# 160 of 544 tokens through gathered expert rows instead of 128, 32 of them packed four heads side by side, with longer runs for what is kept in DRAM

## The reference, cut to what matters

```python
q = einsum('td,de->te', xt, w_q).reshape(t, 8, 2, 128)     # 8 heads, 2 sides
s = einsum('thpc,hpkc->thpk', q, sub_keys)                 # 128 scores a side
s1, i1 = top_k(s[:, :, 0], 16); s2, i2 = top_k(s[:, :, 1], 16)
top_s, j = top_k(s1[..., :, None] + s2[..., None, :], 16)  # of 256 pairs
e = i1[j // 16] * 128 + i2[j % 16]                         # 16 experts a head
gate = softmax(top_s)
act = gelu(einsum('td,thkd->thk', xt, u_experts[e]))
out = einsum('thk,thkd->td', gate * act, v_experts[e])
```

## Time and profile before

| | |
|---|---|
| median of 3 runs | 1608.98 us (1602.33 to 1609.36) |
| the profiled execution | 1603.43 us, its span 1601.3 us |
| TensorE busy | 96% of the span |
| VectorE, ScalarE, GpSimd busy | 76%, 41%, 51% |
| moved by DMA | 407.60 MB, 255 GB/s over the span |
| granted TensorE clock, mean | 0.983 |

### The profile page before, as it was taken

One profiled execution on the slowest core, in us unless ns is written; L12 is line 12 of the kernel. 1 busy time (PEld: TensorE's weight loads), 2 busy tenths in 40 slices (PEclk: granted clock), 3 DMA queues, 4 the chain that ended last, 5 costly groups with the idle time before them and its releaser, 6 DMA issues.

```text
span 1601.3 us, 26951 instructions
## 1 busy us (share of the span) xinstructions
PE 1538.5 (96%) x9360; PEld 1505.2 (94%) x9360; DVE 1223.4 (76%) x2594; ACT 649.9 (41%) x838; POOL 813.6 (51%) x497
## 2 busy tenths in 40 slices
PE   6998889999999989999999998999999999999996
PEld 6997879998999989899999998999999999999996
DVE  6998983788999996777777630677777777787775
ACT  5244443343333344566666523333333333333332
POOL 5686533336667756666676675244344444343301
PEclk9999989999999999999999999999999999999999
DMA  4321212227767767999999997789998998999841
GB/s 165 96 89 53 83 45 102 66 90 250 227 225 245 276 221 245 351 370 363 352 372 372 353 399 265 245 324 355 341 350 326 335 326 318 353 344 345 323 167 56
DMA packets 149503, 407.60 MB, mean 255 GB/s; under 512 B 12224, under 2 KB 75968, under 8 KB 147648
## 3 DMA queue, kind: packets, MB, share of 16 engines
q1 hardware_dynamic: 89776, 215.27, 39.5%
q0 software_dynamic: 36864, 134.23, 22.3%
q10 hardware_dynamic: 22800, 57.42, 9.2%
HBM read 349.99 MB, written 56.89 MB: 254 GB/s over the span
## 4 chain that ended last, share of the span: by engine, by line
PE 86%; DVE 6%; DMA 5%; ACT 2%; issue 1%; POOL 0%; DVEq 0%; SPq 0%; ACTq 0%
PE ps_unit L750 32%; PE ps_unit L810 18%; PE ps_misc L810 18%; PE ps_unit L567 13%; DMA acts_dram<-act_ring 3%; PE ps_misc L784 2%; DMA raw<-stream 1%; DVE mov_lo L1150 1%; PE ps_misc L710 1%; PE ps_unit L642 1%; ACT gates L1061 1%; DVE hid L1270 1%; PE ps_unit L697 0%; DMA hid<-x_t 0%; DMA rows<-u_rows,expert 0%
## 5 line engine op out<-in xcount | busy, mean ns | idle before, releaser
L446 POOL TENSOR_TENSOR w_lo<-raw,w_hi 128x1024 fp32r<-128x1024 f32 x172 | 417.1, 2429 | 300.5 <-ACT w_hi L865 188.8
L750 PE MATMUL ps_unit<-mov_hi,w_hi 128*128 128x416 f32 x1024 | 366.7, 358 | 8.5 <-POOL w_lo L446 8.5
L531 POOL DMA_INDIRECT rows<-v_rows,expert x128 | 207.9, 1624 | 318.0 <-DVE sums L1358 309.2
L750 PE MATMUL ps_unit<-mov_hi,w_lo 128*128 128x416 f32 x1024 | 362.6, 354 | 0.0
L750 PE MATMUL ps_unit<-mov_lo,w_hi 128*128 128x416 f32 x1024 | 360.3, 352 | 0.0
L865 ACT ACTIVATE w_hi<-raw 128x1024 fp32r<-128x1024 f32 x300 | 315.7, 1053 | 89.8 <-ACT act_ring L1033 59.9
L1085 ACT ACTIVATE prod_hi<-prod 128x416 fp32r<-128x416 f32 x128 | 70.7, 552 | 367.1 <-PE ps_misc L810 365.8
L1544 DVE TENSOR_TENSOR prod_lo<-prod,prod_hi 128x416 fp32r<-128x416 f32 x128 | 75.8, 592 | 173.9 <-ACT prod_hi L1085 173.9
L750 PEld LDWEIGHTS ps_unit<-mov_hi,w_hi 128*128 128x128 f32 x1024 | 194.0, 189 | 11.3 <-ACT w_hi L865 5.2
L750 PEld LDWEIGHTS ps_unit<-mov_lo,w_hi 128*128 128x128 f32 x1024 | 194.4, 190 | 2.6
L750 PEld LDWEIGHTS ps_unit<-mov_hi,w_lo 128*128 128x128 f32 x1024 | 193.8, 189 | 1.8
(11 more groups left out here) (213 smaller groups left out, 2739.8 us busy)
## 6 DMA issues: line engine op xcount, KB each, us to landing
raw<-stream SPq DMA_DIRECT2D x300, 512.0 KB, 4.5
acts_dram<-act_ring ACTq DMA_DIRECT2D x128, 208.0 KB, 5.2
gates_dram<-gates ACTq DMA_DIRECT2D x13, 2048.0 KB, 10.7
gates_in<-gates_dram SPq DMA_DIRECT2D x16, 1664.0 KB, 14.8
acts_in<-acts_dram SPq DMA_DIRECT2D x32, 832.0 KB, 7.5
hid<-x_t SPq DMA_DIRECT2D x4, 544.0 KB, 8.0
rows<-u_rows,expert POOLq DMA_INDIRECT x128, 6.9
rows<-v_rows,expert POOLq DMA_INDIRECT x128, 7.6
```

Of the source, the lines that this page charges most:

```text
L446: nc.gpsimd.tensor_tensor(w_lo[:, j, :], raw[:, j, :], w_hi[:, j, :].bitcast(F32), ALU.subtract).then_inc(lo_made, 1)
L531: nc.gpsimd.indirect_dma_start(out=rows[:, n % ROWS_RING, :], out_offset=None, in_=table, in_offset=bass.IndirectOffsetOnAxis(ap=expert[:, ...
L750: last = nc.tensor.matmul(dense_psum(j), w[:, j, k * P:(k + 1) * P], m[:, k, 0:DENSE], start=(k == 0 and n == 0), stop=(k == KC - 1 and n ...
```

## The change

- `GATHERED` is 160: `DENSE` is 384, so 3 dense tiles in place of 4, 12 gate groups in place of 13, and matmuls of 384 columns.
- The 32 new gathered tokens (512 to 543; the other 128 are now 384 to 511) are packed: each stands on 4 groups of 32 partitions, and each group holds 2 of the 8 heads. So they need 32 slots more (`SLOTS` = 160). Their scores come in a fourth PSUM bank, `best_pairs` runs for them once with 2 tiles, after the dense heads. For their dots `x_rows` is overwritten by `x_rows_x` after slot 127. Their weighted rows are added into `sums_x`, first of all v slots (`value_slot`), and at the end the 4 groups are brought together by 4 DMAs and three additions.
- `EARLY_HEADS` is 2, `U_BEFORE` 15, 5 dots in each of 12 gate groups in place of 6 in each of 13; `U_AFTER` stays 5. One `soften` for all tokens in place of two. `fetched_by` follows: 35 dots before the gates, 60 in them, 65 after.
- Activations are spilled in pairs of units from a ring of 4 (runs of 3 KB), gates are loaded for 16 units, in 3 pieces of 4 groups (runs of 2 KB), one group ahead; `product` runs 4 units ahead in place of 3.
- The starting values of `sums` and `sums_x` are transposed after the gates instead of before the u units.

```diff
-GROUP = 8
+GROUP = 16
+QUARTERS = GROUP // QUARTER
+GATE_PIECES = 3
-GATHERED = 128
+GATHERED = 160
+PACKED = GATHERED - P
+PARTS = P // PACKED
+PACKED_HEADS = HEADS // PARTS
-U_BEFORE = 14
+U_BEFORE = 15
-SLOTS = HEADS * TOPK
+WHOLE = HEADS * TOPK
+SLOTS = WHOLE + PACKED_HEADS * TOPK
-EARLY_HEADS = 1
-DOTS_A_GROUP = 6
-DOTS_EARLY = (HEADS - EARLY_HEADS) * DOTS_A_HEAD
+EARLY_HEADS = 2
+DOTS_A_GROUP = 5
+DOTS_EARLY = (HEADS - EARLY_HEADS + 1) * DOTS_A_HEAD
+MADE_AHEAD = AHEAD + 1
+def value_slot(m):
+    return (m + WHOLE) % SLOTS
 def fetched_by(u):
-    n = u - FIRST_U - 8
-    if n < -2:
+    n = u - FIRST_U - 3
+    if n < 3:
         return 0
-    heads = DOTS_A_HEAD * max(7 * n // (RING * U_BEFORE - 6), 0)
-    groups = DOTS_A_GROUP * max(u - FIRST_U - RING * U_BEFORE - 2, 0) // RING
-    return min(min(heads, DOTS_EARLY) + groups, SLOTS) + ROWS_RING
+    early = DOTS_EARLY * min(max(n - 10, 0), RING * U_BEFORE - 10) // (RING * U_BEFORE - 10)
+    groups = DOTS_A_GROUP * min(max(n - RING * U_BEFORE, 0), RING * GTS) // RING
+    late = (SLOTS - DOTS_BEFORE) * max(n - RING * (U_BEFORE + GTS), 0) // (RING * U_AFTER - 3)
+    return min(early + groups + late, SLOTS) + ROWS_RING
...
-            def load_gates(group, s):
-                g = gates_dram[:, :, bass.ds(GROUP * group, GROUP), :].rearrange("g p e t -> p g (e t)")
+            def load_gates(group, s, piece):
+                part = slice(piece * GTS // GATE_PIECES, (piece + 1) * GTS // GATE_PIECES)
+                g = gates_dram[part, :, bass.ds(GROUP * group, GROUP), :].rearrange("g p e t -> p g (e t)")
...
+                for q in range(quarters):
                     sp.wait_ge(prod_made, GROUP * group + QUARTER * (q + 1))
-                    load_acts(2 * group + q + 2, q)
-                    if q and gates_too:
-                        load_gates(group + 2, s)
+                    load_acts(QUARTERS * group + q + 2, q % 2)
+                    if q < GATE_PIECES and gates_too:
+                        load_gates(group + 1, 1 - s, q)
...
+            for j in range(RING):
+                u_unit(N_U // RING - U_AFTER, j)
+                if j == 1:
+                    pe.wait_ge(g_took, BATCHES * GTS)
+                    for bank, at in ((0, DENSE), (2, T - P)):
+                        for k in range(KC):
+                            last = nc.tensor.transpose(ps_misc[:, bank + k // 4, (k % 4) * P:(k % 4 + 1) * P],
+                                                       hid[:, k, at:at + P], ident[:])
+                        last.then_inc(rows_turned, 1)
...
             def u_unit(lap, j, first=False, between=None):
                 split_high(FIRST_U // RING + lap, j + 2)
-                if not first:
-                    act.wait_ge(act_saved[(j + 2) % RING], 16 * (lap + j // 2))
+                if not first and j % 2 == 0:
+                    act.wait_ge(act_saved[j // 2], 16 * lap)
...
-                nc.scalar.activation(act_ring[:, j % 2], dense_psum(j), ACT.Gelu).then_inc(act_took, 1)
-                spill(lap, j)
+                nc.scalar.activation(act_ring[:, j], dense_psum(j), ACT.Gelu).then_inc(act_took, 1)
+                if j % 2:
+                    spill(lap, j // 2)
...
             def dot(n):
                 dve.wait_ge(row_in[n % ROWS_RING], 16 * (n // ROWS_RING + 1))
+                if n == WHOLE:
+                    dve.wait_ge(row_used, WHOLE)
+                    step(nc.vector.tensor_copy(x_rows, x_rows_x[:]))
+                    settle()
...
+            best_pairs(scores_x, PACKED_HEADS, lambda t: TILES * HEADS + t, lambda s: ij_x[:, s],
+                       lambda at: dots_of(HEADS - EARLY_HEADS, at))
+            experts(WHOLE, SLOTS, ij_x[:, 0], ij_x[:, 1])
+            soften()
```

More of the change, by code:

```diff
@@ L398, in _ @@
             for s in range(2):
-                load_gates(s, s)
+                for piece in range(s, GATE_PIECES, 2):
+                    load_gates(0, 0, piece)
                 for j in range(RING):
@@ L707, in head_scores @@
                     pe.wait_ge(scores_took, head)
[L708 to L712, removed]
+                for side in range(2):
+                    for t, at in enumerate(TILE_AT):
+                        nc.tensor.matmul(ps_misc[:, t // 2, (t % 2) * 256 + side * P:(t % 2) * 256 + side * P + P],
+                                         q_ring[:, 2 * s + side, at:at + P], keys[:, 2 * head + side, :],
+                                         start=True, stop=True)
+                    part, at = (head % PARTS) * PACKED, (head // PARTS) * 2 * NKEYS + side * NKEYS
+                    last = nc.tensor.matmul(ps_misc[part:part + PACKED, 2, at:at + NKEYS],
+                                            q_ring[:, 2 * s + side, PACKED_AT:T], keys[:, 2 * head + side, :],
+                                            start=True, stop=True)
                 last.then_inc(scores_done, 1)
-            def key_view(head, s, side):
-                return keys[:, bass.ds(2 * head + side, 1), :].rearrange("p a n -> p (a n)")
             first_queries()
@@ L734, in _ @@
                     head_scores(0, 0)
-            with pe.Fori(1, N_Q // RING) as lap:
+            for lap in range(1, N_Q // RING):
                 for j in range(RING):
@@ L1005, in _ @@
                 if j == 1:
-                    for n, dst in enumerate((x_rows_in, sums)):
+                    for n, dst in enumerate((x_rows_in, x_rows_x)):
                         act.wait_ge(rows_turned, n + 1)
@@ L1052, in _ @@
                     u_unit(lap, j)
-                    if lap == 1 and j == 0:
-                        exponents(0, DTILES, TILES)
-            exponents(1, 0, DTILES)
+            act.wait_ge(shifted, 1)
+            nc.scalar.activation(gate[:], gate[:], ACT.Exp).then_inc(exp_made, 1)
             for j in range(RING):
@@ L1369, in best_pairs @@
                 at_of = [best_at[:, t, s] for t, s in rows_of]
-                top_of = [tops[:, (t0 + t) * HEADS + head] for t in tiles]
+                top_of = [tops[:, top_at(t)] for t in tiles]
                 settle_for_max()
@@ L1547, in _ @@
             dots_to(SLOTS)
-            for v in range(AHEAD):
+            for v in range(MADE_AHEAD):
                 product(v)
@@ L1561, in _ @@
             for v in range(N_V):
-                if v < N_V - AHEAD:
-                    product(v + AHEAD)
+                if v < N_V - MADE_AHEAD:
+                    product(v + MADE_AHEAD)
                 if v == FIRST_SUM - 1:
                     dve.wait_ge(gelu_made, 1)
-                    dve.wait_ge(gate_made, 2)
-                    nc.vector.tensor_tensor(weight[:], gelu[:],
-                                            gate[:, DTILES * HEADS:].rearrange("p h k -> p (h k)"),
-                                            ALU.mult).then_inc(weight_made, 1)
+                    dve.wait_ge(gate_made, 1)
+                    whole = slice(DTILES * HEADS, TILES * HEADS)
+                    packed = slice(TILES * HEADS, GATE_ROWS)
+                    for a, b, of in ((0, WHOLE, whole), (WHOLE, SLOTS, packed)):
+                        last = nc.vector.tensor_tensor(weight[:, a:b], gelu[:, a:b],
+                                                       gate[:, of].rearrange("p h k -> p (h k)"), ALU.mult)
+                    last.then_inc(weight_made, 1)
+                    dve.wait_ge(rows_in_made, 4)
                     dve.wait_ge(weight_made, 1)
```

239 lines of the change are left out of this document (148 added, 91 removed).

## The result

| | |
|---|---|
| changed kernel, median of 7 runs | 1618.2 us (1611.48 to 1625.1) |
| kernel before, 7 runs beside them | 1602.33 us (1597.83 to 1609.36) |
| ratio | 1.0088, 95% interval 1.0063 to 1.0113 |
| span of the profiled execution | 1614.4 us (before 1601.3) |

A forecast was written before the change was run, and what follows sets the result against it. TensorE, 96% busy, was taken as the bound, with transfers near full as a second. v beginning at 1014 plus 558 gave 1572, profiled execution 1574, named median 1577, 32 us less; range 1547 to 1609.

The forecast's parts named there:

- The matmuls: All u and v matmuls: 384 columns take 14.6 ns less each, over 6144 matmuls 89.7 us saved.
- u units alone: Stage of 60 u units before the gates: 273 us, so the gates begin at 616.5 (before 612.3).
- the hole: TensorE's wait while GpSimd stands for the experts, then does eight fetches and a split: 17 us, before 3.6.
- The gates: Stage of 12 gate groups: 21.0 us each, matmuls and bytes both near that bound, 252 us in all; ScalarE's spill waits go.
- The last 20 u units: Stage before v: 65 dots left instead of 15, GpSimd as good as fully busy, last dot at 1002; matmul saving buys nothing.
- The rival of a slow clock there: Last u laps: TensorE idles 3 us a unit and falls to half clock, 17 us more, 1594; chance 0.13.
- The chain behind the last dot: Between last u dot and first v matmul: products, splits, unit 127 and a GELU take 12 us; v starts at 1014.
- The v stage: v and the end: 594.3 less 44.9 for matmuls plus 9 for transfers and bursts, 4.25 us a unit, 558 us.
- The sign that I had named: v stage: the forecast is wrong if TensorE has holes there that end at `prod`, `prod_lo` or `w_lo`.
- The packed rows' last additions: End of v stage: 3 + 1 operations of some 1.2 us fall into units without row sums and cost nothing.
- The cap near 365 GB/s: Rival: transfers cap the v stage, 4.48 us a unit, 36 us in place of 9, 1617; chance 0.2.
- The rival of the third piece: v stage: third gate piece late, or VectorE fails to hide; 25 to 30 us more, 1605; chance 0.12.

The follow-up runs named there:

- u_later: v_order, with GpSimd waiting for the experts and sending the first eight fetches after splitting u unit FIRST_U + 9 instead of + 6: 1564.63 us.
- before_pairs: Kernel before, with only activations spilled in pairs of units from a ring of 4 and read back in longer runs: 1594.65 us, ratio 0.9939.
- u_spread: v_order, with 8 dots in place of 5 in each head's routing, so 44 dots instead of 65 in the last u laps: 1554.46 us.
- v_order: Changed kernel, with the last two weight loads of a v lap issued after the next quarter's activation and gate loads instead of before: 1574.77 us, ratio 0.9818.
- v_ahead3: Changed kernel, with product running 3 units ahead, as before the change, instead of 4: 1573.6 us, one run.
- v_short_stream: Changed kernel, with v weight units from the third lap on loaded only in 576 of 1024 columns: 1591.12 us, one run.
- v_gates_first: Changed kernel, with all three pieces of the next group's gates sent at the first quarter of a group: 1630.75 us, one run.

## Why the prediction was wrong

*The matmuls* were right: 173.2 ns for 173.6 where nothing holds TensorE up.

*u units alone*: 276.8 for 273. The mechanism of the hole is as told. Timeline of GpSimd in the changed kernel, beside the earlier trace rows:

```profile
369.72 2.40 POOL L480 TENSOR_TENSOR w_lo<-raw,w_hi 128x1024 fp32r<-128x1024 f32 x1 [2.40 <-issue]
381.81 1.13 POOL L567 DMA_INDIRECT rows<-u_rows,expert  x1 [9.69 <-ACT w_hi L913]
...
390.72 0.94 POOL L567 DMA_INDIRECT rows<-u_rows,expert  x1 [0.30 <-issue]
391.68 7.02 POOL L480 TENSOR_TENSOR w_lo<-raw,w_hi 128x1024 fp32r<-128x1024 f32 x3
```

GpSimd has split at 372.1 and stands 9.7 us; then come the eight fetches and the split. The experts were made at 381.2, for my 379.5. TensorE's hole was 14.0 us, for my 17. `u_later` moved this wait and got 10 us: the hole is 4.0 us there. That the stage still took 4 us more than forecast lies partly in matmuls 175.3 ns apart for 173.6 (2.5 us); the rest is open.

*The gates*: 250 for 252. I had said that the waits for spills go; `before_pairs` puts 9 us on that part of the change.

*The last 20 u units*: 141 for 145.5, at 386 GB/s. That rows left over set the pace is shown by `u_spread`, 28 us for 21 rows. Whether GpSimd's time (7.3 us a unit) or the bytes are the nearer limit stays open: both fall with the rows, and no run moved one alone. GpSimd was not "as good as fully busy", with 105 of the 140 us, and from 874 to 1004 us VectorE waited 48.6 us for rows to land while the queues carried 399 GB/s; that leans to the bytes. The rival of a slow clock there was half right, at a mean of 0.87, but the stage was no longer than forecast. The chain behind the last dot came as told, 12 us: dots end at 1003.7, v begins at 1015.6.

*The v stage* is the step that failed: "I take 4.25, nearer to 400 [...] and the rest is for bursts". The bytes and the rate hold (393 GB/s at 4.16 us a unit in `v_order`), and VectorE's share nearly does (3.9 us busy a unit for 3.8). What I priced at 9 us was the lead of the loads, and its loss cost 40 (598.8 for the 558.4 of `v_order`): by the gaps in the two traces about 26 us in holes, the rest in the slow clock behind them, for which I had set nothing in this stage. I had worked out that the third piece of gates has 4 units, 17 us, against a landing time of 14.8. The trace of the changed kernel has 7 us at that place. I counted from the condition that SyncE waits for (`prod_made`) and left out what stands ahead of it in SyncE's order, four weight loads of 14 us. The timeline of SyncE in the kernel before shows them too:

```profile
1196.91 15.32 SPq L370 DMA_DIRECT2D raw<-stream  x4
1212.70 0.38 SPq L377 DMA_DIRECT2D acts_in<-acts_dram  x1
1213.30 0.38 SPq L382 DMA_DIRECT2D gates_in<-gates_dram  x1
```

And I read "`product` runs 4 units ahead in place of 3" in the diff without a price: it asks for activations and gates one unit sooner while their issue hangs on the weight splits. `v_ahead3` and `v_order` each lengthen that lead on their own, by one unit and by two, and each takes the whole loss away. The sign that I had named came true: TensorE's holes end at `w_lo`.

That `v_order` comes to 558.4, just the forecast's 558, is partly luck. Its units take 4.16 us, so the 9 us were not spent on them. They went elsewhere: "The packed rows' last additions [...] fall into units without row sums, so nothing" was wrong too. In `v_order` they hold VectorE ahead of the last weight split, and TensorE stands 5.6 us for it (in the changed kernel as well, at 1578.6). VectorE, then TensorE:

```profile
1531.27 3.59 DVE L1675 TENSOR_TENSOR rows<-rows 32x1024 f32<-32x1024 f32 x3
1534.89 1.21 DVE L1677 CUSTOM_DVE_ANT_0 rows<-rows 32x1024 f32<-32x1024 f32 x1
...
1536.04 1.21 DVE L1568 TENSOR_TENSOR w_lo<-raw,w_hi 128x1024 fp32r<-128x1024 f32 x1
```

```profile
1537.30 0.69 PE L860 MATMUL ps_unit<-prod_hi,w_hi 128*128 128x384 f32 x1 [5.60 <-DVE w_lo L1568]
```

And from the last start of a v matmul to the end pass 17.6 us, for 13.1 before; no run says why. A smaller slip: 1574 and 5.6 give 1580 for the median, and I named 1577.

*The rivals.* The cap near 365 GB/s would have given 1617, almost the time measured, and it is refuted: `v_order` carries 393 at a share of 1.00, and `v_short_stream` keeps the late gates at 325. In the changed kernel 364 GB/s was the result of VectorE's standing still, not its cause. By the Trainium skill (DMA: Bandwidth & Descriptors, "Specifications"), about 358 GB/s is a core's limit to HBM; with one core at work, 393 over 400 us disagrees. The rival of the third piece (7 boundaries of 4 us, chance 0.12) was the nearest: about 26 us of holes did come, at the starts of groups. It left out the activations, which came late as well, and the slow clock behind each hole.

## What to carry to other kernels

A prefetch has as much lead as lies between its issue and its use, and in an in-order queue the issue comes when everything ahead of it has stopped waiting: read both times in the trace before saying that a transfer is hidden. Running a consumer further ahead takes lead from its inputs; here one unit of 4.2 us made the difference between 1574 and 1618 us, a kernel about 30 us faster than before or one 16 us slower, with 6 to 10% to spare on VectorE instead of 22% and the queues near full. In this stage the slow clock behind the holes cost about half of what the holes themselves did; a price for a wait of TensorE has to include it. A DMA rate that looks like a ceiling can be the echo of a stall: ask whether it stays when bytes are taken away.

## What the runs showed that I had not expected

The 16 DMA engines carried 393 GB/s for 400 us beside a TensorE without a hole. A load queue near its limit is sensitive to order alone: `v_gates_first` takes 53 us more than `v_order` for the same bytes (v 611.7 for 558.4). After the hole of 14 us TensorE ran 4.7 us at a granted clock of about 0.5 (1.2 GHz). Timeline of TensorE, changed kernel:

```profile
394.20 0.66 PE L789 MATMUL ps_unit<-mov_hi,w_hi 128*128 128x384 f32 x1 [14.03 <-POOL w_lo L480]
...
398.49 0.52 PE L789 MATMUL ps_unit<-mov_lo,w_hi 128*128 128x384 f32 x1
398.81 0.38 PE L789 MATMUL ps_unit<-mov_hi,w_lo 128*128 128x384 f32 x1
399.03 0.34 PE L789 MATMUL ps_unit<-mov_hi,w_hi 128*128 128x384 f32 x1
399.20 0.33 PE L789 MATMUL ps_unit<-mov_lo,w_hi 128*128 128x384 f32 x1
```

The starts are 320 ns apart up to 398.8 and 174 from 399.0 on, so this hole cost 2 us more than its own length.
